# A mixture-of-experts decoder step: where the gather of the next expert's tokens stands in TensorE's order

## What is computed

```python
logits = xt @ w_router + b_router
top_val, top_idx = lax.top_k(logits, TOP_K)          # TOP_K = 4 of 32
gates = softmax(top_val)
# for every expert e, over the tokens that chose it:
g = minimum(xblk @ w_gate[e] + b_gate[e], 7.0)
u = clip(xblk @ w_up[e] + b_up[e], -7.0, 7.0)
a = (u + 1.0) * (g * sigmoid(1.702 * g))
y = a @ w_down[e] + b_down[e]                         # weighted by the gate, added to the token's row
```

## Time and profile before

| | |
|---|---|
| median of 3 runs | 1242.43 us (1241.77 to 1242.64) |
| time of the profiled execution | 1242.96 us |
| its span, first to last instruction | 1241.1 us |
| TensorE matmuls busy | 1198.1 us, 97% |
| VectorE busy | 492.5 us, 40% |
| ScalarE busy | 186.7 us, 15% |
| TensorE's mean granted clock | 0.996 |
| moved by DMA | 461.29 MB, mean 372 GB/s |

### The profile page before, as it was taken

One profiled execution on the slowest core, in us unless ns is written; L12 is line 12 of the kernel. 1 busy time (PEld: TensorE's weight loads), 2 busy tenths in 40 slices (PEclk: granted clock), 3 DMA queues, 4 the chain that ended last, 5 costly groups with the idle time before them and its releaser, 6 DMA issues.

```text
span 1241.1 us, 15077 instructions
## 1 busy us (share of the span) xinstructions
PE 1198.1 (97%) x5648; PEld 487.8 (39%) x5648; DVE 492.5 (40%) x1189; ACT 186.7 (15%) x394; POOL 10.0 (1%) x13
## 2 busy tenths in 40 slices
PE   8999989999999999999999999999999999999997
PEld 5665654555333333333333333333233333333332
DVE  2399872345432334323332333333343333332323
ACT  3204443133100010100000000000010010010002
POOL 0000000000000000000000000000000000000000
PEclk9999999999999999999999999999999999999999
DMA  9925557829999999999999999999999999999994
GB/s 346 339 80 160 182 189 280 348 91 389 373 393 426 429 425 427 427 428 427 428 427 427 428 428 428 426 427 428 427 426 427 427 426 428 426 425 428 427 425 170
DMA packets 53476, 461.29 MB, mean 372 GB/s; under 512 B 6313, under 2 KB 16361, under 8 KB 27495
## 3 DMA queue, kind: packets, MB, share of 16 engines
q1 hardware_dynamic: 51407, 450.55, 87.9%
q0 software_dynamic: 1152, 8.39, 1.9%
q10 hardware_dynamic: 864, 1.64, 0.4%
HBM read 457.64 MB, written 3.28 MB: 371 GB/s over the span
## 4 chain that ended last, share of the span: by engine, by line
PE 74%; DMA 20%; DVE 4%; issue 1%; ACT 1%; ACTq 0%; SPq 0%; DVEq 0%
PE psum L914 40%; DMA ring<-in_w_up 17%; PE psum L892 6%; PE psum L364 5%; PE psum L956 4%; PE psum L429 3%; DMA ring<-in_w_gate 3%; PE psum L640 2%; DVE ring L1844 2%; PE psum L413 1%; PE psum L768 1%; PE psum L556 1%; PE psum L775 1%; PE psum L600 1%; PE psum L402 1%
## 5 line engine op out<-in xcount | busy, mean ns | idle before, releaser
L914 PE MATMUL psum<-ring,work 128*64 128x512 f32 x3056 | 672.8, 594 | 21.4 <-DMA ring<-in_w_up 20.4
L914 PEld LDWEIGHTS psum<-ring,work 128*64 128x64 f32 x3056 | 214.9, 137 | 468.1 <-issue 413.2
L892 PE MATMUL psum<-H,work 128*64 128x512 f32 (+1 forms) x384 | 92.7, 600 | 0.0
L2281 DVE TENSOR_TENSOR work<-psum,keep 128x512 f32<-128x512 f32 x16 | 11.1, 692 | 158.8 <-PE psum L914 158.8
L1844 DVE SCALAR_TENSOR_TENSOR ring<-ring,extra 128x256 f32<-128x256 f32 x240 | 74.0, 386 | 0.1
L2267 DVE TENSOR_TENSOR X<-X,psum 128x512 f32<-128x512 f32 x63 | 43.2, 686 | 64.6 <-PE psum L956 64.5
L2281 DVE TENSOR_TENSOR work<-psum,work 128x512 f32<-128x512 f32 x16 | 11.1, 692 | 139.9 <-PE psum L914 139.8
L1701 ACT COPY work<-psum 64x512 f32<-64x512 f32 x32 | 18.5, 578 | 296.6 <-PE psum L914 296.6
L1689 ACT COPY work<-psum 128x512 f32<-128x512 f32 x31 | 18.2, 586 | 277.3 <-PE psum L892 277.3
L1680 ACT ACTIVATE work<-work 128x512 f32<-128x512 f32 x32 | 20.1, 629 | 227.8 <-DVE work L2357 227.8
L364 PEld LDWEIGHTS psum<-C,work 128*128 128x128 f32 (+1 forms) x330 | 44.4, 194 | 22.9 <-issue 19.5
(11 more groups left out here) (345 smaller groups left out, 960.7 us busy)
## 6 DMA issues: line engine op xcount, KB each, us to landing
ring<-in_w_gate SPq DMA_DIRECT2D x64, 2048.0 KB, 25.5
ring<-in_w_down SPq DMA_DIRECT2D x63, 2048.0 KB, 29.8
ring<-in_w_up SPq DMA_DIRECT2D x61, 2048.0 KB, 28.4
ring<-in_cache_keys SPq DMA_DIRECT2D x64, 144.0 KB, 3.0
ring<-in_w_in SPq DMA_DIRECT2D x1, 4096.0 KB, 25.8
ring<-in_mem_keys_turned SPq DMA_DIRECT2D x8, 512.0 KB, 14.1
ring<-in_cache_mem_v SPq DMA_DIRECT2D x8, 512.0 KB, 7.5
ring<-in_w_in SPq DMA_DIRECT2D x1, 2688.0 KB, 19.4
```

The costliest lines, as they stand in the source:

```text
L892: last = mm(psum[64 * nh:64 * nh + 64, 2, :], Ph[0:ROWS[tt], tt, :], xn[0:ROWS[tt], tt, 512 * nh:512 * nh + 512], start=tt == 0, stop=tt == 2)
L914: last = mm(psum[64 * nh:64 * nh + 64, bank, :], src[:, j, 64 * half:64 * half + 64], w[:, j, 512 * nh:512 * nh + 512], start=first and j ...
L2281: v.tensor_tensor(gm, psum[:, 0, :], B[b][:, 0:512], ALU.add).then_inc(s.g_sum, 1)
```

## The change

In the first four experts `gather` of the next expert's tokens is called behind the gate product (and behind the scatter and, in expert 0, `job_lists`), ahead of the up product. The four transposes of the gathered tokens (`turn(3, XG, ...)`) are called right behind the up product, ahead of the scatter. Nothing is added or removed, and the order on VectorE, ScalarE and SyncE's queue is the same. The loops and the experts from 4 on are as before.

```diff
-            def expert(i, q, first=False, since=None, last_one=False):
+            def expert(i, q, first=False, since=None, between=False, last_one=False):
...
                     if since == 1:
                         scatter_again(t, pairs * 5 + 5)
-                if not last_one:
+                    if t == 0 and between:
+                        pe.wait_ge(s.p_built, e + 2)
+                        gather(s.xg_full)
+                if between:
+                    pe.wait_ge(s.xg_moved, e + 2)
+                    turn(3, XG, s.xt_full)
+                elif not last_one:
                     pe.wait_ge(s.p_built, e + 2)
                     gather(s.xg_full)
...
                 pe.wait_ge(s.a_ready, e + 1)
                 turn(4, AA, s.at_full)
-                if not last_one:
+                if not last_one and not between:
                     pe.wait_ge(s.xg_moved, e + 2)
                     turn(3, XG, s.xt_full)
...
             for q in range(4):
-                expert(0, q, first=q == 0)
+                expert(0, q, first=q == 0, between=True)
```

## The result

| | before | changed |
|---|---|---|
| runs | 10 | 10 |
| median | 1242.02 us | 1249.22 us |
| lowest to highest | 1240.89 to 1244.44 us | 1245.33 to 1256.63 us |

The ratio is 1.0057, 95% interval 1.0038 to 1.0077: slower by 7.2 us at the medians, clear of the 0.2% that can be told. The sign was forecast (0.82 for slower). The median lies 0.3 us above the range, and the runs spread over 11 us, which was not forecast at all. Two things have to be explained: what is slower in every run, and what differs from run to run.

A forecast was written before the change was run, and what follows sets the result against it. The weight stream was taken to bound most experts, TensorE the early stretch; 2.16 + 0.34 + 0.99 = 3.49 us of waits plus 1.6 us of clock gave 5.1 us, so 1247.5 us, range 1244.8 to 1248.9 us.

The forecast's parts named there:

- the range: Whole kernel time: 1244.8 to 1248.9 us, from the kept clock at its lower bounds to late slots with half that spread.
- What bounds the kernel: Over most experts the full weight stream sets the pace; delays of experts 0 and 1's down products move the rest one for one.
- The delays of experts 2 and 3: Delays of 0.34 and 0.99 us again, falling on TensorE while the weight stream is full, so costing nothing.
- The wait for the plan: Expert 0's gather, now ahead of the up product, waits for VectorE's plan of expert 1: TensorE stands still 2.16 us.
- The AA transposes: Behind the up product they lose the gather as cover: 0.34 us lost in even experts, 0.99 us in odd ones.
- The late up slots: Up slots come free 2.82 us later, 4.98 in expert 0; gaps in the stream absorb it: 0, bounds 0 and 1.0 us.
- The clock: TensorE's granted clock falls behind expert 0's standstill, costing 1.6 us in its gather and up product; chance 0.47.
- the clock stays: Rival: granted clock stays 1.00 behind expert 0's standstill, all waits unchanged; price 3.5 us, 1245.9 us; chance 0.27.
- The rule of the Trainium skill: Only gaps clearly longer than expert 0's standstill reset TensorE's clock; sum 3.5 instead of 5.1 us.
- No slower than can be told: Rival: waits behind experts 0 and 1's up products are covered; under 2.5 us slower or not at all; chance 0.15.
- The gaps do not take up the late up slots: Rival: late weight loads for experts 2 and 3 push their successors; up to 1.0 us on top, 1248.5 us; chance 0.08.
- Faster: Rival: needs a slot freed earlier, but no product in experts 0 to 3 begins earlier; only run spread; chance 0.03.

The follow-up runs named there:

- again3: The changed kernel run once more with no edit, against the kernel before: 1246.89 us against 1242.61, ratio 1.0037.
- filled: The changed kernel with 8 calls of small matmuls in expert 0's standstill, against the kernel before: 1246.18 us against 1242.49, ratio 1.0034.
- again: The changed kernel run again with no edit, against the kernel before: 1247.2 us against 1243.25, ratio 1.0033.
- before3: The kernel before with no edit, one more profile: 1240.72 us.
- first_only: The kernel before with the new order in expert 0 alone: 1245.5 us against 1243.25, ratio 1.0016.
- turn_late: The changed kernel with the gathered tokens' transposes back behind those of AA, against the kernel before: 1246.52 us against 1242.49, ratio 1.0032.
- plan_early: The changed kernel with expert 1's plan built on VectorE ahead of the routing lists, against the kernel before: 1244.09 us against 1242.49, ratio 1.0014.
- without_first: The kernel before with the new order in experts 1 to 3 alone, against the kernel before: 1244.73 us, ratio 0.9998.
- again4: The changed kernel with no edit, one more profile of expert 0: single run of 1248.09 us.
- before2: The kernel before with no edit, one more profile: 1247.76 us.

## Why the prediction was right and wrong

*What bounds the kernel* was right. Column F is 880.7 to 882.9 us in 14 profiles while E runs from 53.3 to 61.7: what expert 3's gate 0 is late by is what the end is late by, and nothing else of the change arrives there. The delays of experts 2 and 3 left no trace, as forecast: in the mean of the ten profiles with the new order in experts 1 to 3 F is 0.2 us above the first profile of the kernel before, and in the other four 0.1.

*The wait for the plan*, forecast 2.16 us: the gather begins 11.20 us behind the first gate product where the up product began at 9.11, so 2.09 us (again3). *The AA transposes*: forecast 0.34 and 0.99; C less that 2.09 is 0.31, and D is 1.00. The sums agree better than the way to them. In again3 only 0.16 of the 0.31 and 0.85 of the 1.00 stand between the end of the up product and the down product; the other 0.15 in each is that the up product (in expert 0 also the gather) takes a little longer in its new place, which was put at nothing. And TensorE's matmuls are idle for 0.58 us in the odd experts and not at all in the even ones, where 1.0 and 0.4 us were forecast as a sign: the transposes of the gathered tokens, the scatter and `turn_gates` fill the rest. Only a weight load waits for `AA` in expert 0, for 0.23 us. *The late up slots*: forecast 0, and E less (B + C + D) is 0.00 to 0.01 in all profiles. The sum without the clock was forecast at 3.49 us; again3 and filled show 3.40.

*The clock* is where it was wrong, in two places: in the price of the fall behind the standstill, and in taking that for the only fall that could differ from run to run. The first step was "Its price is read from 16 matmuls that took 8.80 us across such a fall": 1.6 us, once, taken to be the case. That is a price for one low stretch of 3.4 us, and one of the five profiles shows it (4.05 - 2.40 = 1.65). Three show twice that, 3.3 us, since the clock was low for some 7 us, through the gather and into the up product. One shows none. I had read a single size from a single earlier fall, and the same rows gave no reason why a fall should not last twice as long. (The same 16 matmuls take 7.10 or 7.11 us in profiles where the clock stays up there, again, before3, again3 and first_only, so one such fall costs 1.7 us and not 1.6.) The case "the clock stays" with 3.5 us is a real one too, and was rightly kept as a rival.

*The range* failed at the second place, and this is what put the median above it. It took the spread of three runs of the kernel before, 0.9 us, so falls of the clock outside the changed place were put at nothing. The three happened to be alike; the kernel before spreads over 9 us in the later runs. A fifth of its runs have a low mean clock and take some 5 us longer, and the one profile among them has a long low stretch at 118 us. Of the first ten runs of the changed kernel five were of this kind. They lie at 1250.08 us and above, the other five at 1248.37 and below (median 1245.96, 3.9 us above the kernel before), and 1249.22 is the middle between two groups and not a time that a run had. In both later comparisons the median, 1247.2 and 1246.89 us, is within the forecast range.

Some 4 to 5 us of the 7.2 are the change. By the times it is 4.1 and 4.6 us in the two later comparisons (0.0033 and 0.0037 of 1243), and 4.0 between the groups of high clock, 1246.5 less 1242.5. The five profiles give more, 3.4 us in each and 0, 1.65 or 3.3 of clock in expert 0, 5.7 in the mean. But the profiled executions are slow ones of their groups: 1256.63 us is the highest of all 36, and the other four (1249.12, 1248.52, 1248.09 and 1247.06) are above the median of the 24 with high clock. So a typical run loses less to the clock in expert 0 than the profiles show, and how often it loses what there is open. The forecast of 5.1 us is then near the cost, partly by luck: the fall was charged to every run, and not every run has it. What is left of the 7.2 I put down to the share of runs with the early stretch; why the first ten runs had so many is not shown.

*The rule of the Trainium skill* (page "TensorE: Matmul & The Clock Gate", section "HAM oscillation — how this bites in real kernels"), that only clearly longer gaps put the clock back, would have given 1245.9 us. Four of five profiles of the changed kernel have the clock low behind 2.03 us of idle time, and the measurement decides against it. The fifth, again3, is the case of the rule, with C + D = 3.40 us.

*The rivals.* "The clock stays" is the case of again3 and turn_late, two of seven profiles with the standstill. "No slower than can be told" fell. It needed AA's wait to be covered, and plan_early and without_first show 1.0 us of it in expert 1. "The gaps do not take up the late up slots" fell by column E. "Faster" had nothing for it and did not come.

No version here beats the kernel before. The best of the new order, plan_early, keeps 1.3 us of loss in its profile.

## What to carry to other kernels

Moving work from behind a product to ahead of it changes no busy time, but it takes away a cover: list what waited unseen behind the moved work (here VectorE's 2.2 us between the up product and the transposes), and ask for each place where the work lands whether its own input is ready in the first, irregular round, not only in the steady one. A new idle time of TensorE of about 2 us has a price beyond its length, and a range, not a number: here 0, 1.65 or 3.3 us. Look whether the runs fall into groups before you read their median, and how many of each group there are. Where a stream of loads is full for most of the kernel, find the last gap in it, and cost a change by what it does to the load that ends that gap; the rest can be left out.

## What the runs showed of the hardware

An idle time of the same length, 2.03 us behind the same instructions, was followed by a low clock in four profiles of the changed kernel and in first_only, and not in again3 and turn_late. Its length is not enough to tell. Pauses in code that no run changed show the same:

| idle time of TensorE | profiles | low clock behind it |
|---|---|---|
| 2.00 to 2.41 us before L402 | 4 | 4 |
| 1.16 to 1.79 us before L402 | 6 | 0 |
| 1.77 to 1.79 us before the later L600 | 10 | 5 |
| 1.68 to 1.70 us before the first L600 (1.44 in again4) | 14 | 4 |
| 1.53 us before L1072, at some 945 us | 14 | 6 |
| 0.97 to 1.00 us before L364, at some 115 us | 14 | 4 |

(Line numbers of the kernel before.) The low clock begins up to 1.8 us after the end of the pause, in a few profiles within it; in the last row it begins 2.0 to 2.5 us after, and whether that pause has a part in it is not shown. The prediction had one profile, in which 1.69 us left the clock up and 1.78 us did not. It looked like a border between two lengths; over 14 profiles a pause of 1.53 us can be followed by a fall and one of 2.03 us by none.

The low stretches had different lengths: 3.4 us (again4, first_only), some 7 us (three profiles), and some 13 to 14 us at 117 to 131 us, behind an idle time of only 0.99 us before L364 in before2. The same 0.99 us stands in the first profile of the kernel before, without a fall. So a kernel on one core can have two groups of times, here 5 us apart; what the profiles of the slower group have in common, and the others do not have, is that early stretch of low clock. Three runs need not show it.
